# The triangular solve of an RWKV-7 time mix: summing by rows instead of updating what is left

## The chip, the cores and the metric

The kernel runs on one core of one Trainium2 chip. The core has TensorE (PE, matrix products), VectorE (DVE), ScalarE (ACT), GpSimd (POOL) and SyncE (SP, here the queue that issues the transfers). The metric is device microseconds of one execution, and the median of several runs is given.

## The reference

Two model blocks are computed one after the other for 256 tokens of width 1024, in float32: the first with attention, a gated spatial mixer and expert lookups, the second with SwiGLU layers, a parallel attention and, in its second layer, an RWKV-7 time mix. Only the last bears on the change. Its recurrence, over 16 heads of 64, is:

```
def rwkv7_step(state, inp):
    r_t, w_t, k_t, v_t, a_t, b_t = inp
    sa = jnp.einsum('bhvk,bhk->bhv', state, a_t)
    state = (state * w_t[:, :, None, :] + sa[..., None] * b_t[:, :, None, :]
             + v_t[..., None] * k_t[:, :, None, :])
    return state, jnp.einsum('bhvk,bhk->bhv', state, r_t)
```

## The kernel before, in words

The kernel does not step through 256 tokens. It cuts them into 8 chunks of 32 (`C = 32`; 4 chunks in each of two tiles of 128 tokens). Inside a chunk, what a token adds to the state depends on the earlier tokens of the chunk through a strictly triangular 32 x 32 matrix of products. For each of the 16 heads and 8 chunks, 128 systems in all, the kernel needs the inverse of identity minus that matrix. `invert` (L2237 to L2308) computes them all at once, one system on each of the 128 partitions.

The order of `invert` is written out by hand and is the same on every run. Transposes and matmuls on TensorE give the products, VectorE masks them into `sysd`. Then a block of instructions begins in which only SyncE and VectorE take part. SyncE stores `sysd` to a buffer in memory and loads it back as `sy`, now with one system a partition (L2284). VectorE meanwhile clears `XT`, writes ones on its diagonal, and clears `inv`. Then comes the solve (L2299 to L2308). `XT[p, j, t]` becomes the inverse of system p, `sy[p, i, t]` is its matrix, nonzero for i < t. The tiles are row-major with 32 float32 to a row, so neighbours in t are 4 bytes apart and neighbours in i or j 128 bytes. In the trace `sy` is called sys and `inv` is called inverseT.

Step i of the solve takes column i of `XT`, which is final by then, and adds its product with row i of `sy` to all later columns. That is one multiplication into `terms` (L2302) and one addition into `XT` (L2304). `kit.dve` makes VectorE wait for the end of an instruction before the next one starts. The last addition signals `solved`. SyncE waits for it, stores `XT` (L2286), waits for that, and loads the inverses as diagonal blocks of `inv` (four loads). All engines meet at the end of the block. Then `vector_only` clears a state (L1984), and `recur` runs twice, once for each tile of 128 tokens, with `inv` as an operand of its matmuls. `finish_mix` follows, and one more SwiGLU ends the kernel.

Of the kernel before, what the change touches and what calls it, by code (L numbers as in the profile page):

```python
# [18 lines left out]
ALU = mybir.AluOpType  # L19
ACT = mybir.ActivationFunctionType  # L20
AX = mybir.AxisListType.X

P = 128
# [30 lines left out]
C = 32  # L54
# [160 lines left out]
def transposes(kit, jobs):  # L215


    nc = kit.nc
    turned, freed = kit.count("turned"), [kit.count("turned_out_act"), kit.count("turned_out_dve")]
    b0, f0 = turned.n, [f.n for f in freed]  # L220
    with nc.Block() as block:
        @block.tensor
        def _(pe):
            for j, (ins, _) in enumerate(jobs):
                if j >= 4:
                    pe.wait_ge(freed[j % 2].sem, f0[j % 2] + (j - 4) // 2 + 1)
                n = ins[0].shape[0]
                for i, a in enumerate(ins):
                    mm = nc.tensor.transpose(kit.bank[j % 4][:, i * n:(i + 1) * n], a, kit.ident[0:n, 0:n])
                turned.up(mm)  # L230

        def source(j):
            n, t = len(jobs[j][0]), jobs[j][0][0].shape[0]
            return kit.bank[j % 4][:, 0:n * t].rearrange("p (n t) -> p n t", n=n)

        @block.scalar
        def _(act):
            for j in range(0, len(jobs), 2):
                act.wait_ge(turned.sem, b0 + j + 1)
                freed[0].up(nc.scalar.copy(jobs[j][1], source(j)))  # L240

        @block.vector
        def _(dve):
            for j in range(1, len(jobs), 2):
                dve.wait_ge(turned.sem, b0 + j + 1)
                freed[1].up(nc.vector.tensor_copy(jobs[j][1], source(j)))
# [1990 lines left out]
def invert(kit, dram, A, KK, inv):  # L2237

    nc = kit.nc
    NS = NT * RH
    grams, masked, stored, loaded, solved = (kit.count(n) for n in ("grams", "grams_masked", "systems_stored", "loaded",
                                                                    "solved"))
    g0, m0, t0, l0, v0 = grams.n, masked.n, stored.n, loaded.n, solved.n
    tri, out = (dram[n].rearrange("(u c) (j t) -> c j u t", c=CH, j=C) for n in ("systems", "inverses"))
    with kit.sb("sysd", [P, NS, C]) as sysd, kit.sb("sys", [P, C, C]) as sy, kit.sb("XT", [P, C, C]) as XT, \
            kit.sb("terms", [P, C, C]) as terms:
        with kit.sb("aT", [P, NT * KD, P]) as aT, kit.sb("bT", [P, NT * KD, P]) as bT:
            transposes(kit, [([src[:, T, (k + i) * P:(k + i + 1) * P] for i in range(4)],  # L2250
                              dst[:, T * KD + k:T * KD + k + 4, :])
                             for src, dst in ((KK, aT), (A, bT)) for T in range(NT) for k in (0, 4)])
            with nc.Block() as block:
                @block.tensor
                def _(pe):


                    for n in range(NS // 4):
                        if n >= 4:
                            pe.wait_ge(masked.sem, m0 + (n - 3) * CH)  # L2260
                        for i in range(4):
                            b, p = n % 2 * HD, n // 2 * 4 + i
                            mm = nc.tensor.matmul(kit.bank[n % 4][:, i * P:(i + 1) * P], bT[b:b + HD, p, :],
                                                  aT[b:b + HD, p, :], start=True, stop=True)
                        grams.up(mm)

                @block.vector
                def _(dve):
                    for n in range(NS // 4):
                        dve.wait_ge(grams.sem, g0 + n + 1)  # L2270
                        for c in range(CH):
                            r = slice(c * C, (c + 1) * C)
                            bank = kit.bank[n % 4][:, :].rearrange("p (u t) -> p u t", u=4)
                            u = n // 2 * 8 + n % 2
                            masked.up(nc.vector.tensor_tensor(sysd[r, u:u + 7:2, :], bank[r, :, r],
                                                              kit.lt[r, r].unsqueeze(1).to_broadcast([C, 4, C]), ALU.mult))

        with nc.Block() as block:
            @block.sync
            def _(sp):  # L2280
                for c in range(CH):
                    stored.up(sp.dma_start(tri[c], sysd[c * C:(c + 1) * C]), 16)
                sp.wait_ge(stored.sem, t0 + 16 * CH)
                kit.load(sp, sy[:], dram["systems"].rearrange("s (j t) -> s j t", j=C))  # L2284
                sp.wait_ge(solved.sem, v0 + 1)
                stored.up(sp.dma_start(dram["inverses"].rearrange("s (j t) -> s j t", j=C), XT[:]), 16)  # L2286
                sp.wait_ge(stored.sem, t0 + 16 * (CH + 1))
                for c in range(CH):
                    r = slice(c * C, (c + 1) * C)
                    kit.load(sp, inv[r, :, r], out[c])  # L2290
                sp.wait_ge(loaded.sem, l0 + 16 * (CH + 1))

            @block.vector
            def _(dve):
                kit.dve(nc.vector.memset(XT[:], 0.0))
                kit.dve(nc.vector.memset(XT[:].rearrange("p j t -> p (j t)")[:, 0::C + 1], 1.0))
                nc.vector.memset(inv[:], 0.0)
                dve.wait_ge(loaded.sem, l0 + 16)
                for i in range(C - 1):  # L2299

                    n, later = C - 1 - i, XT[:, 0:i + 1, i + 1:]
                    kit.dve(nc.vector.tensor_tensor(terms[:, 0:i + 1, 0:n], XT[:, 0:i + 1, i].unsqueeze(2).to_broadcast([P, i + 1, n]),  # L2302
                                                    sy[:, i, i + 1:].unsqueeze(1).to_broadcast([P, i + 1, n]), ALU.mult))
                    ins = nc.vector.tensor_tensor(later, later, terms[:, 0:i + 1, 0:n], ALU.add)  # L2304
                    if n > 1:
                        kit.dve(ins)
                    else:
                        solved.up(ins)  # L2308
# [326 lines left out]
```

## Time and profile before

| | |
|---|---|
| median of 3 runs | 3264.07 us (3259.56 to 3265.90) |
| the profiled execution | 3264.07 us, span 3262.2 us |
| mean granted TensorE clock | 0.895 of full speed |
| TensorE matmuls busy | 2546.1 us (78%) |
| VectorE busy | 1768.1 us (54%) |
| ScalarE busy | 1103.9 us (34%) |
| GpSimd busy | 594.6 us (18%) |

A busy share is an average over stages with different limits. What a change in one stage is worth is read from that stage: from the timeline of its stretch, and from who waits for whom there. All positions in time are microseconds from the start of the span.

### The profile page before, as it was taken

The page shows a single profiled execution, that of the slowest core. Times are in us where ns is not written, and L with a number is a line of the kernel's source. Part 1 is how long each engine was busy: PE and PEld are TensorE (multiplying, and loading weights), DVE is VectorE, ACT ScalarE, POOL GpSimd, SP SyncE. Part 2 cuts the span into 40 slices and gives each one's busy share as a digit, 9 for nine tenths or more (in the row PEclk, how much of TensorE's full clock was granted, in tenths as well). Part 3 has the DMA queues.
Part 4 walks back from the last instruction along what each step waited for, and adds up shares of the span by engine and source line. Part 5 has one row for each costly group of instructions (what it writes and reads, how often), then busy time and mean ns, then how long its engine had stood idle before and what let it go on. Part 6 is the DMA issues. An engine that isn't in the chain of part 4 may idle for free. (4 is left out here: it accounts for less than half of the span.)

```text
span 3262.2 us, 35838 instructions
## 1 busy us (share of the span) xinstructions
PE 2546.1 (78%) x13519; PEld 1769.7 (54%) x13519; DVE 1768.1 (54%) x3125; ACT 1103.9 (34%) x2207; POOL 594.6 (18%) x516
## 2 busy tenths in 40 slices
PE   6776788888874787888777988479989785285899
PEld 4554333333223333333226978359979782185798
DVE  3325866666554866666654544325544454645454
ACT  3232434444332444444334333333333241100332
POOL 0001444444420444444430000000000000000000
PEclk8877999999996999999998999669989887575899
DMA  9755999999982999999992544115535432100353
GB/s 376 272 198 213 418 421 422 421 421 419 415 342 87 419 421 421 421 421 421 421 421 101 186 168 156 42 45 181 188 140 181 160 137 80 26 1 14 114 190 116
DMA packets 134224, 817.07 MB, mean 250 GB/s; under 512 B 24863, under 2 KB 32375, under 8 KB 38348
## 3 DMA queue, kind: packets, MB, share of 16 engines
q0 software_dynamic: 73728, 536.90, 39.7%
q1 hardware_dynamic: 60364, 278.47, 23.6%
q8 instruction: 76, 1.25, 0.2%
q14 instruction: 56, 0.46, 0.0%
HBM read 813.16 MB, written 2.16 MB: 250 GB/s over the span
## 5 line engine op out<-in xcount | busy, mean ns | idle before, releaser
L1241 PE MATMUL bank<-rows,diag 128*128 128x512 f32 x2048 | 998.6, 621 | 259.6 <-ACT diag L1304 259.2
L1423 DVE CUSTOM_DVE_ANT_0 rows<-rows,h 128x1024 f32<-128x1024 f32 x512 | 623.8, 1227 | 424.1 <-DMA rows<-in_peer_rows,idx 420.3
L1241 PEld LDWEIGHTS bank<-rows,diag 128*128 128x128 f32 x2048 | 365.2, 193 | 814.3 <-ACT diag L1304 522.1
L1191 POOL DMA_INDIRECT rows<-in_peer_rows,idx x512 | 594.4, 1161 | 1113.1 <-PE bank L1241 688.6
L1627 DVE TENSOR_TENSOR low<-weight_ring,high 128x2048 fp32r<-128x2048 f32 x132 | 301.5, 2292 | 275.7 <-ACT high L1602 275.7
L1559 PE MATMUL bank<-hT_high,low 128*128 128x256 f32 x1408 | 403.4, 287 | 0.0
L1559 PE MATMUL bank<-hT_low,high 128*128 128x256 f32 x1408 | 402.8, 286 | 0.0
L1559 PE MATMUL bank<-hT_high,high 128*128 128x256 f32 x1408 | 402.7, 286 | 0.0
L1295 ACT ACTIVATE picks<-picks 128x1 f32<-128x1 f32 x512 | 103.5, 202 | 739.0 <-DVE picks L1423 733.5
L1602 ACT CAST high<-weight_ring 128x2048 fp32r<-128x2048 f32 x132 | 250.5, 1903 | 264.5 <-PE bank L1559 132.1
L1559 PEld LDWEIGHTS bank<-hT_high,low 128*128 128x128 f32 x1408 | 274.8, 195 | 7.4 <-issue 4.5
L1559 PEld LDWEIGHTS bank<-hT_low,high 128*128 128x128 f32 x1408 | 274.7, 195 | 1.4
L1559 PEld LDWEIGHTS bank<-hT_high,high 128*128 128x128 f32 x1408 | 274.5, 195 | 0.0
L1304 ACT ACTIVATE diag<-const_table,picks 128x128 f32<-128x128 f32 x512 | 205.5, 401 | 48.3 <-ACT picks L1299 1.5
L1299 ACT ACTIVATE picks<-picks 128x1 f32<-128x1 f32 x512 | 150.7, 294 | 18.5
L1217 PE MATMUL bank<-x_high,low 128*128 128x256 f32 x256 | 114.8, 449 | 29.9 <-DVE low L1334 24.5
L1574 PE MATMUL bank<-low,hidden 128*128 128x512 f32 x352 | 137.6, 391 | 0.0
L1574 PE MATMUL bank<-high,hidden_low 128*128 128x512 f32 x352 | 137.5, 391 | 0.0
L1574 PE MATMUL bank<-high,hidden 128*128 128x512 f32 x352 | 137.0, 389 | 0.0
L477 PE MATMUL bank<-low,x_high 128*128 128x256 f32 x432 | 126.3, 292 | 11.8 <-DVE low L489 11.8
L477 PE MATMUL bank<-high,x_low 128*128 128x256 f32 x432 | 124.5, 288 | 0.0
L477 PE MATMUL bank<-high,x_high 128*128 128x256 f32 x432 | 124.2, 287 | 0.0
(412 smaller groups left out, 3268.4 us busy)
## 6 DMA issues: line engine op xcount, KB each, us to landing
weight_ring<-in_ffn_w_gate SPq DMA_DIRECT2D x44, 1024.0 KB, 4.8
weight_ring<-in_ffn_w_up SPq DMA_DIRECT2D x44, 1024.0 KB, 4.8
weight_ring<-in_ffn_w_down SPq DMA_DIRECT2D x44, 1024.0 KB, 4.8
mod_ring<-in_mod_w SPq DMA_DIRECT2D x40, 1024.0 KB, 7.9
weight_ring<-in_peer_w_q SPq DMA_DIRECT2D x16, 1024.0 KB, 7.5
weight_ring<-in_attn_w_in SPq DMA_DIRECT2D x12, 1024.0 KB, 4.8
weight_ring<-in_mod_w SPq DMA_DIRECT2D x8, 1024.0 KB, 16.9
rows<-in_peer_rows,idx POOLq DMA_INDIRECT x512, 15.1
```

Of the source, the lines that this page charges most:

```text
L477: mm = nc.tensor.matmul(o, t[:, k, cols], w[:, k, :], **kw)
L1191: nc.gpsimd.indirect_dma_start(ring[:, s], None, dram["peer_rows"], bass.IndirectOffsetOnAxis(ap=idx[:, T, n:n + 1], axis=0)).then_inc(row ...
L1217: mm = nc.tensor.matmul(kit.bank[hh % 2][:, half * SEQ:(half + 1) * SEQ], w[:, k, half * P:(half + 1) * P], t[:, k, :], start=(k == 0 and ...
L1241: mm = nc.tensor.matmul(bank[:, :], diag[:, j % DIAG_SLOTS], ring[:, j % ROW_SLOTS, D + half * 512:D + (half + 1) * 512], start=(hh == 0 a ...
L1295: gelued.up(nc.scalar.activation(dot[:, T, n:n + 1], dot[:, T, n:n + 1], ACT.Gelu_apprx_tanh))
L1299: scaled.up(nc.scalar.activation(weight[:, T, n:n + 1], dot[:, T, n:n + 1], ACT.Copy, scale=gate[:, T, n:n + 1]))
L1304: weighed.up(nc.scalar.activation(diag[:, j % DIAG_SLOTS], kit.ident, ACT.Copy, scale=weight[:, T, n:n + 1]))
L1423: dotted.up(nc.vector.tensor_tensor_reduce(out=ring[:, s, 0:D], in0=ring[:, s, 0:D], in1=h[:, T], scale=1.0, scalar=0.0, op0=ALU.mult, op1 ...
L1559: mm = nc.tensor.matmul(o, w[:, k, s * P:(s + 1) * P], t[:, k, :], start=(k == 0 and n == 0), stop=(k == KD - 1 and n == 2))
L1574: mm = nc.tensor.matmul(kit.bank[4 + 2 * T + half][:, :], hidden[:, f % 2, s, T * P:(T + 1) * P], w[:, s, half * 512:(half + 1) * 512], st ...
L1602: nc.scalar.copy(hi, w).then_inc(high_made.sem, 1)
L1627: nc.vector.tensor_tensor(lo, w, hi.bitcast(F32), ALU.subtract).then_inc(split.sem, 1)
```

## The change

Step i used to update all columns behind column i. Now step t makes column t final in one go: it multiplies the finished t x t corner of `XT` with column t of `sy`, repeated down the rows, and sums the products of each row into column t of `XT`. There are still 31 multiplications, each followed by one more instruction in the same chain of waits. The second is a `tensor_reduce` along the innermost dimension in place of a `tensor_tensor`. Loads, stores, memsets and the signal `solved` are as before.

```diff
-                for i in range(C - 1):
-
-                    n, later = C - 1 - i, XT[:, 0:i + 1, i + 1:]
-                    kit.dve(nc.vector.tensor_tensor(terms[:, 0:i + 1, 0:n], XT[:, 0:i + 1, i].unsqueeze(2).to_broadcast([P, i + 1, n]),
-                                                    sy[:, i, i + 1:].unsqueeze(1).to_broadcast([P, i + 1, n]), ALU.mult))
-                    ins = nc.vector.tensor_tensor(later, later, terms[:, 0:i + 1, 0:n], ALU.add)
-                    if n > 1:
+                for t in range(1, C):
+
+                    kit.dve(nc.vector.tensor_tensor(terms[:, 0:t, 0:t], XT[:, 0:t, 0:t],
+                                                    sy[:, 0:t, t].unsqueeze(1).to_broadcast([P, t, t]), ALU.mult))
+                    ins = nc.vector.tensor_reduce(XT[:, 0:t, t], terms[:, 0:t, 0:t], AX, ALU.add)
+                    if t < C - 1:
                         kit.dve(ins)
                     else:
                         solved.up(ins)
```

The start of the solve on VectorE, before (in these rows a shape such as 128x2x30 is partitions, rows, elements of a row):

```order
L2297 MEMSET inverseT 128x4096
L2302 TENSOR_TENSOR terms<-XT,sys 128x31
L2304 TENSOR_TENSOR XT<-XT,terms 128x31
L2302 TENSOR_TENSOR terms<-XT,sys 128x2x30
L2304 TENSOR_TENSOR XT<-XT,terms 128x2x30
L2302 TENSOR_TENSOR terms<-XT,sys 128x3x29
```

And now:

```order
L2297 MEMSET inverseT 128x4096
L2301 TENSOR_TENSOR terms<-XT,sys 128x1
L2303 TENSOR_REDUCE XT<-terms 128x1
L2301 TENSOR_TENSOR terms<-XT,sys 128x2x2
L2303 TENSOR_REDUCE XT<-terms 128x2
L2301 TENSOR_TENSOR terms<-XT,sys 128x3x3
```

The blocks began wide and flat and now begin small. The shape of a reduction is that of its output; it reads as many elements as the multiplication ahead of it writes. The end of the solve, before:

```order
L2302 TENSOR_TENSOR terms<-XT,sys 128x29x3
L2304 TENSOR_TENSOR XT<-XT,terms 128x29x3
L2302 TENSOR_TENSOR terms<-XT,sys 128x30x2
L2304 TENSOR_TENSOR XT<-XT,terms 128x30x2
L2302 TENSOR_TENSOR terms<-XT,sys 128x31
L2304 TENSOR_TENSOR XT<-XT,terms 128x31
L2278 UNCONDITIONAL_BRANCH
```

And now:

```order
L2301 TENSOR_TENSOR terms<-XT,sys 128x29x29
L2303 TENSOR_REDUCE XT<-terms 128x29
L2301 TENSOR_TENSOR terms<-XT,sys 128x30x30
L2303 TENSOR_REDUCE XT<-terms 128x30
L2301 TENSOR_TENSOR terms<-XT,sys 128x31x31
L2303 TENSOR_REDUCE XT<-terms 128x31
L2278 UNCONDITIONAL_BRANCH
```

The blocks used to get narrow again and now are largest at the end. The rows around the solve, and those of all other engines, are as they were, one line of the kernel further up.

## Rows read from the trace of the kernel before

**Rows 1.** Timeline of the solve: start us, us, instruction, [idle before].
```profile
2811.30 3.47 DVE L2297 MEMSET inverseT<- 128x4096 f32 x1 [0.92 <-DVE XT L2296]
2814.10 0.34 SPq L172 DMA_DIRECT2D sys<-systems  x1
2817.31 0.19 DVE L2302 TENSOR_TENSOR terms<-XT,sys 128x31 f32<-128x31 f32 x1 [2.54 <-DMA sys<-systems]
2817.54 0.19 DVE L2304 TENSOR_TENSOR XT<-XT,terms 128x31 f32<-128x31 f32 x1
...
2840.46 0.21 DVE L2304 TENSOR_TENSOR XT<-XT,terms 128x31 f32<-128x31 f32 x1
2840.70 0.34 SPq L2286 DMA_DIRECT2D inverses<-XT  x1
2843.32 2.17 SPq L172 DMA_DIRECT2D inverseT<-inverses  x4
2849.00 0.48 DVE L1984 MEMSET states<- 128x512 f32 x1 [8.33 <-PEq L2278]
...
2849.79 0.45 PE L229 MATMUL bank<-const_table,KK 128*128 128x128 f32 x1 [44.68 <-PEq L1949]
```
**Rows 2.** The same stretch as one row of windows: length, busy by engine, clock, DMA.
```profile
2817.31:2840.67 23.36, 0.00 (x0) 0.00 (x0) 21.27 (x62) 0.00 (x0) 0.00 (x0) 0.50 0.00 0
```
**Rows 3.** Waits of SyncE and TensorE around it: us, times, longest.
```profile
SPq L2286 <- DVE XT L2304: 26.2, 1, 26.2
...
PE bank L229 <- PEq L1949: 44.7, 1, 44.7
```
**Rows 4.** Groups by shape, first step of the solve: busy us, mean ns.
```profile
L2302 DVE TENSOR_TENSOR terms<-XT,sys 128x31 f32<-128x31 f32 x1 | 0.2, 193 | 2.5 <-DMA sys<-systems 2.5
L2304 DVE TENSOR_TENSOR XT<-XT,terms 128x31 f32<-128x31 f32 x1 | 0.2, 192 | 0.0
```
**Rows 5.** Groups by shape, widest steps.
```profile
L2302 DVE TENSOR_TENSOR terms<-XT,sys 128x255 f32<-128x255 f32 x2 | 0.9, 426 | 0.1
L2302 DVE TENSOR_TENSOR terms<-XT,sys 128x256 f32<-128x256 f32 x1 | 0.4, 424 | 0.0
```
**Rows 6.** Groups by shape, reductions elsewhere in the kernel.
```profile
L1373 DVE TENSOR_REDUCE ranks<-hT 128x32 f32<-128x512 f32 x28 | 19.2, 686 | 1.0
L1373 DVE TENSOR_REDUCE ranks<-hT 128x16 f32<-128x256 f32 x8 | 3.4, 420 | 0.3
L1388 DVE TENSOR_REDUCE ranks<-picks 128x2 f32<-128x32 f32 x14 | 2.5, 181 | 0.0
L2488 DVE TENSOR_REDUCE st<-sq 128x16 f32<-128x1024 f32 x2 | 2.4, 1220 | 0.1
L1388 DVE TENSOR_REDUCE ranks<-picks 128x1 f32<-128x16 f32 x4 | 0.7, 164 | 0.0
```
**Rows 7.** Groups by shape, memsets ahead of the solve.
```profile
L2297 DVE MEMSET inverseT<- 128x4096 f32 x1 | 3.5, 3472 | 0.9 <-DVE XT L2296 0.9
L2295 DVE MEMSET XT<- 128x1024 f32 x1 | 0.9, 912 | 0.6 <-PEq L2253 0.6
L2296 DVE MEMSET XT<- 128x32 f32 x1 | 0.1, 85 | 0.1
```
**Rows 8.** Timeline of VectorE in `finish_mix`.
```profile
2996.33 1.23 DVE L2498 TENSOR_TENSOR R<-R,G 128x1024 f32<-128x1024 f32 x1
2997.59 1.22 DVE L2484 TENSOR_REDUCE st<-R 128x16 f32<-128x1024 f32 x1
2998.84 0.17 DVE L2485 TENSOR_SCALAR st<-st 128x16 f32<-128x16 f32 x1
```
**Rows 9.** Groups by shape, the last step and the addition before it.
```profile
L2304 DVE TENSOR_TENSOR XT<-XT,terms 128x60 f32<-128x60 f32 x1 | 0.2, 223 | 0.0
L2304 DVE TENSOR_TENSOR XT<-XT,terms 128x31 f32<-128x31 f32 x1 | 0.2, 212 | 0.0
L2302 DVE TENSOR_TENSOR terms<-XT,sys 128x31 f32<-128x31 f32 x1 | 0.2, 210 | 0.0
```
**Rows 10.** The addition of the second step, by shape.
```profile
L2304 DVE TENSOR_TENSOR XT<-XT,terms 128x60 f32<-128x60 f32 x1 | 0.2, 221 | 0.0
```
**Rows 11.** Windows: the two halves of the recurrence (busy PE, PEld, DVE, ACT, POOL, clock).
```profile
2849.79:2914.99 65.20, 58.71 (x769) 55.88 (x769) 27.79 (x43) 4.49 (x8) 0.00 (x0) 0.75 0.01 2
2914.99:2984.05 69.06, 62.82 (x768) 59.61 (x768) 27.88 (x43) 4.52 (x9) 0.00 (x0) 0.69 0.01 2
```
**Rows 12.** Timeline of SyncE's queue behind the solve.
```profile
2984.41 0.42 SPq L172 DMA_DIRECT2D ln<-in_rw_lnx_b  x1
3029.47 0.33 SPq L198 DMA_DIRECT2D weight_ring<-in_ffn_w_gate  x1
```

## The prediction

> **What bounds the kernel now.** I read five views in turn. First the time: the profiled execution took 3264.07 us around a span of 3262.2 us, and it is also the median of the three runs shown (3259.56 to 3265.90). So a sum made on the profile is a sum on the median. What a measurement of this kernel can tell from no change is about 0.2%, 6.5 us.
>
> Second, the timeline of the solve [rows 1]. The reader is to see a single file. VectorE is the only engine at work from 2817.31 to 2840.67 us, first mult to last add. Its first multiplication waits for the load of the systems, the last addition releases the store of the inverses, that store the four loads, those the next stage, whose first matmul starts at 2849.79. Third, the same stretch as one row [rows 2]: 23.36 us, of which VectorE is busy 21.27 in 62 instructions, with DMA share 0.00. Fourth, the waits of the store queue and of TensorE [rows 3]: SyncE waits 26.2 us for the last addition, TensorE 44.7 us at the barrier of the stage. Nothing is prefetched or multiplied beside this stretch. So a microsecond more or less on VectorE there is a microsecond of the span, whatever VectorE's 54% over the whole kernel suggests. Fifth, the durations by shape, for the prices.
>
> **The change, part by part.** Before, step i multiplies and adds a block of (i+1) x (31-i) elements per partition, for i = 0 to 30. After, step t multiplies a block of t x t and sums it by rows, for t = 1 to 31. Both have 31 multiplications and 31 second instructions in one dependent chain. Elements per pass: before, the sum of (i+1)(31-i), 5456; after, the sum of t squared, 10416. So nothing is saved in instructions, and 4960 elements are added in each of two passes.
>
> *Multiplication, fixed part and rate.* 31 elements in adjacent places take 193 ns [rows 4], 255 take 426 [rows 5]: 233/224 = 1.04 ns an element, on a fixed 161 ns. The old passes worked out by that are 2 x (31 x 0.161 + 5456 x 0.00104) = 21.33 us, against 21.27 in [rows 2], so the fit holds for every shape in between, square ones (16 x 16, 424 ns) included. The new multiplications: 31 x 0.161 + 10416 x 0.00104 = 15.82 us, if the operands' layout costs nothing.
>
> *The sum by rows.* The kernel has reductions elsewhere [rows 6]: 256 elements to 16 take 420 ns, 512 to 32 take 686, 1024 to 16 take 1220. From the first to the last that is 800/768 = 1.04 ns an element on 153 ns. Small ones lie a little under (16 to 1: 164 ns, 32 to 2: 181). Rows of 16 and of 64 have one rate, so I see no price per row. 31 x 0.153 + 10416 x 0.00104 = 15.58 us. The rows bound it on both sides to a few tenths. The sums are written down a column, every 32nd element. The nearest row for such a write is the memset of the diagonal, every 33rd element: 32 elements in 85 ns, where the memset of 1024 takes 912 and that of 4096 takes 3472, 0.83 ns an element on 59, which makes 86 for 32 [rows 7]. A strided write costs nothing there, and there is only one to t elements read.
>
> *Gaps.* Before, 23.36 - 21.27 = 2.09 us lie in the 61 gaps, 34 ns each. Elsewhere the next instruction starts some 30 ns after the end, behind a reduction as behind a multiplication [rows 8]. Again 2.1 us, within 0.3.
>
> Sum without layout: 15.82 + 15.58 - 21.27 = +10.1 us.
>
> *The column that is read.* The old multiplication reads a row of the systems, 31 neighbours. The new one reads a column of it, sy[:, 0:t, t], whose elements lie 128 bytes apart, and it is the innermost dimension. No instruction before does that at length, but the last step does it once with 31 elements. Its multiplication reads column 30 of XT and takes 210 ns, where the first step has 193 for 31 neighbours; its addition reads two columns and takes 212 for 192 [rows 4, 9]. With 30 rows of 2 there is no price: that addition takes 223 ns, against 221 with 2 rows of 30 [rows 9, 10]. I read the 17 ns as a price per element, 17/31 = 0.55 ns, about half of the normal rate again. From below: if it is a fixed start-up, 31 x 17 ns = 0.5 us in all. From above: if some of it was hidden in so short an instruction, a full second element time may be due for each, 10416 x 1.04 ns = 10.8 us. I take the nearest row, 10416 x 0.55 = 5.7 us.
> The Trainium skill has both readings. "SBUF — State Buffer", section "Door 1: The DMA port swizzle", says that two accesses to a 16-byte line are needed for full bandwidth and that each crossing to a new line costs; the trace agrees, as the 31 x 1 form pays [rows 9] and the 30 x 2 form doesn't. "VectorE: DVE Perf Modes", section "Mode 1× (REGULAR) — the baseline", says of that mode that fp32 and odd strides work and that it gives one result a cycle; by that the column is free.
>
> *The rest.* The diagonal, the memsets, the store and the four loads stay: 2840.70 to 2849.79 is only shifted. The SyncE queue holds nothing but this chain; the next weight load is issued at 3029.47 [rows 12], behind the recurrence. TensorE idles before the recurrence 16 us longer, from a granted clock already at 0.50 [rows 2], the low level of 1.2 GHz; it can't go lower there. So I price this at nothing but a shift of phase, priced below with the rivals.
>
> Forecast: 3264.07 + 10.1 + 5.7 = 3279.9 us, slower by 0.48%. The likeliest case's own range is 3276 to 3284: the two terms have some 1 us between them (20 ns instead of 17 would be 6.7 us), and the rest is the clock.
>
> **The rivals.**
>
> *A, the column is free.* The 17 ns are a start-up for strided forms, or belong to rows of one element. For it: it is one instruction of 31 elements, and the strided write is free [rows 7]. Against: the addition, with two strided reads, shows 20 ns also. The time is 3264.07 + 10.1 to 10.6, 3274.4.
>
> *B, the column costs a whole element time or more.* For it: in 31 elements some of the price can lie in the fixed 161 ns. Against: nothing was hidden in the memset, whose rate fits at 32 elements. 3264.07 + 10.1 + 10.8 = 3285 us.
>
> *C, the clock gives it back, and the kernel is faster.* The two halves of the recurrence do the same work, but took 65.20 us at a mean granted clock of 0.75 and 69.06 at 0.69 [rows 11]. So the clock's phase is worth about 4 us a half, and the change shifts that phase. To offset 15.8 us and reach -6.5, TensorE's busy time of 58.7 + 62.8 = 121.5 us would have to fall by 22.4. Taken as scaling with the clock, it is 58.7 x 0.75 + 62.8 x 0.69 = 87.4 us of full clock, so the mean clock would have to be over 87.4/99.1 = 0.88 in both halves; at 1.0 the time would be 3264.07 + 15.8 - 34 = 3246 us. Against: both halves are far under 0.88 and nothing in the change makes TensorE's work there denser. A partial case, both halves as the better one or better still, takes 4 to 8 us off, and with a free column it would end within 0.2%: about 3268.
>
> *D, the change does not do what it says*, since the stretch is hidden elsewhere: [rows 3] excludes it.
>
> **How the numbers follow.** Forecast 0.5, A 0.24, B 0.17, the partial case of C (within 0.2%) 0.07, C in full 0.02. All but C are slower by more than 0.2%: 0.91; the same 0.07; faster 0.02. Time 3280. The range takes in A with 3 us of scatter below and B: 3270 to 3287; left out are C and what lies beyond B, under 2 in 10.
>
> **What would show it.** The solve as 38 to 40 us between its first multiplication and its last sum, where there were 23.36, still 62 instructions; the store right behind. The sum over 31 x 31 elements at 1.15 us. The multiplication over 31 x 31 at 1.16 us if A holds, 1.7 if the forecast does (161 + 961 x 1.59), 2.2 with B. In the recurrence, halves of 65 to 69 us as before. I am wrong if the reductions cost per row (small t far over 0.2 us), if that stretch does not account for the difference of the spans within 5 us, or if the difference is under 6.5 us.

## The result: slower by 0.58%

The changed kernel takes 3282.35 us (median of 10 runs; 3278.45 to 3292.96 in nine of them; the tenth took 7244.23 us, for a reason that nothing here shows, and is left aside). The kernel before, run beside it, takes 3265.43 (10 runs, 3256.21 to 3274.36). The ratio is 1.0058, with a 95% interval of 1.0041 to 1.0076: 13 to 25 us slower. 3280 were forecast. The profiled execution took 3286.17 us around a span of 3284.3.

In the profile after, the solve is the same single file, only longer. The same stretch as one row of windows (length, busy PE, PEld, DVE, ACT, POOL, clock, DMA share, GB/s), to be set beside [rows 2]:

```profile
2817.65:2858.02 40.37, 0.00 (x0) 0.00 (x0) 38.26 (x62) 0.00 (x0) 0.00 (x0) 0.50 0.00 0
```

40.37 us for 23.36, so +17.0 us, with 62 instructions as before. The gaps are 40.37 - 38.26 = 2.1 us, as before. The waits that answer to [rows 3] (us, times, longest) have grown by the same amount, 17.0 and 17.5:

```profile
SPq L2286 <- DVE XT L2303: 43.2, 1, 43.2
...
PE bank L229 <- PEq L1949: 62.2, 1, 62.2
```

Its end in the timeline (start us, us, instruction, idle before) shows that what follows at once is shifted and not changed. The store follows the last sum, the loads 2.6 us later, and the first matmul comes 9.3 us behind the issue of the store, where it was 9.1 [rows 1]:

```profile
2855.03 1.79 DVE L2301 TENSOR_TENSOR terms<-XT,sys 128x961 f32<-128x961 f32 x1
2856.86 1.16 DVE L2303 TENSOR_REDUCE XT<-terms 128x31 f32<-128x961 f32 x1
2858.04 0.34 SPq L2286 DMA_DIRECT2D inverses<-XT  x1
2860.66 2.28 SPq L172 DMA_DIRECT2D inverseT<-inverses  x4
...
2867.32 0.45 PE L229 MATMUL bank<-const_table,KK 128*128 128x128 f32 x1 [62.16 <-PEq L1949]
```

The groups by line over the solve (busy us, mean ns) split the 38.26 us. Before, the two groups had 10.6 us each.

```profile
L2301 DVE TENSOR_TENSOR terms<-XT,sys 128x1 f32<-128x1 f32 (+30 forms) x31 | 22.6, 730 | 3.6 <-DMA sys<-systems 2.6
L2303 DVE TENSOR_REDUCE XT<-terms 128x1 f32<-128x1 f32 (+30 forms) x31 | 15.6, 505 | 1.1
```

The reductions are where the sum put them, at 15.6 us. The multiplications are at 22.6. The sum had 15.8 for elements in rows and 5.7 for the column. By shape:

```profile
L2301 DVE TENSOR_TENSOR terms<-XT,sys 128x961 f32<-128x961 f32 x1 | 1.8, 1789 | 0.0
L2303 DVE TENSOR_REDUCE XT<-terms 128x31 f32<-128x961 f32 x1 | 1.2, 1155 | 0.0
...
L2301 DVE TENSOR_TENSOR terms<-XT,sys 128x256 f32<-128x256 f32 x1 | 0.6, 585 | 0.0
...
L2303 DVE TENSOR_REDUCE XT<-terms 128x16 f32<-128x256 f32 x1 | 0.4, 422 | 0.0
```

A multiplication of 256 elements took 424 ns in the old 16 x 16 step [rows 5] and takes 585 now. 961 take 1789: (1789 - 161)/961 = 1.69 ns an element, where the reduction of the same block has 1.04.

The span of this execution grew by 22.1 us, not by 17.0. Of the other 5.1, 0.3 lie ahead of the solve and 4.5 between the store of the inverses and the next load on SyncE's queue, 147.82 us for 143.31. The instructions there are the same; "The clock behind the solve" below takes this up.

### The profile page after: what moved, and what is told of

Read it like the earlier page. It is cut to its first block and busy times, and to the rows that moved or that the text cites. A ratio compares the mean times of both kernels' runs of the same rounds, so it can differ in the third digit from the quotient of the medians.

```text
span 3284.3 us, 35838 instructions
## 1 busy us (share of the span) xinstructions
PE 2553.2 (78%) x13519; PEld 1775.5 (54%) x13519; DVE 1784.7 (54%) x3125; ACT 1104.5 (34%) x2207; POOL 595.5 (18%) x516
## 5 line engine op out<-in xcount | busy, mean ns | idle before, releaser
L1304 ACT ACTIVATE diag<-const_table,picks 128x128 f32<-128x128 f32 x512 | 205.5, 401 | 48.3 <-ACT picks L1299 1.5
```

Source lines behind the costliest of these rows:

```text
L1304: weighed.up(nc.scalar.activation(diag[:, j % DIAG_SLOTS], kit.ident, ACT.Copy, scale=weight[:, T, n:n + 1]))
```

## The experiments

Theory 1: the kernel is slower by what VectorE does in the solve, 10.1 us for more elements and the rest for the column, a price of about 0.65 ns for each element of an operand whose neighbours are 128 bytes apart. Rivals: the surplus belongs to the square blocks or the column write; it is a start-up for each instruction; or part of the time comes from the clock behind the solve.

In all of them the solve is read from the profile, from the first multiplication to the end of the last instruction of the solve. In the diffs, `...` stands for lines left out.

**The column taken away.** In the changed kernel the operands of the matmul that makes the systems are exchanged, and the mask is the other triangle:

```diff
-                            mm = nc.tensor.matmul(kit.bank[n % 4][:, i * P:(i + 1) * P], bT[b:b + HD, p, :],
-                                                  aT[b:b + HD, p, :], start=True, stop=True)
+                            mm = nc.tensor.matmul(kit.bank[n % 4][:, i * P:(i + 1) * P], aT[b:b + HD, p, :],
+                                                  bT[b:b + HD, p, :], start=True, stop=True)
...
-                                                              kit.lt[r, r].unsqueeze(1).to_broadcast([C, 4, C]), ALU.mult))
+                                                              kit.after[r, r].unsqueeze(1).to_broadcast([C, 4, C]), ALU.mult))
...
-                                                    sy[:, 0:t, t].unsqueeze(1).to_broadcast([P, t, t]), ALU.mult))
+                                                    sy[:, t, 0:t].unsqueeze(1).to_broadcast([P, t, t]), ALU.mult))
```

> The changed kernel, but the two operands of the matmul that makes the systems are exchanged and the mask is the opposite triangle, so that each system lies transposed in memory and the multiplication reads a row of it, sy[:, t, 0:t], 4 bytes apart. Everything else, t x t blocks and sums by rows written down a column, is as changed. Theory 1 (the column that is read costs some 0.65 ns an element, as 31 x 31 elements took 1.789 us): the multiplication over 31 x 31 falls to 1.16 us, the solve from 40.4 us to 33.5, and the time is 10 us over the kernel before. Theory 2 (the surplus over 1.04 ns an element belongs to the square blocks or to what the column write of XT leaves behind): the multiplication stays at 1.7 to 1.8 us and the solve at 40 us, 17 us over.

The solve took 33.53 us. In the window of the solve, and by shape:

```profile
2820.14:2853.67 33.53, 0.00 (x0) 0.00 (x0) 31.42 (x62) 0.00 (x0) 0.00 (x0) 0.50 0.00 0
```
```profile
L2301 DVE TENSOR_TENSOR terms<-XT,sys 128x961 f32<-128x961 f32 x1 | 1.2, 1160 | 0.0
L2303 DVE TENSOR_REDUCE XT<-terms 128x31 f32<-128x961 f32 x1 | 1.2, 1155 | 0.0
```

The multiplications fell from 22.6 to 15.8 us: the column's price is 6.8 us, 0.65 ns for each of the 10416 elements. What is left, 33.53 - 23.36 = 10.2 us, is the price of the larger blocks and of the sum in place of the addition, forecast at 10.1. The ratio to before is 1.0030 (1.0010 to 1.0051), 3 to 17 us over before, which holds 10.

**The column given to the kernel before.** The same exchange and mask in the kernel before, and a column in its multiplication:

```diff
-                                                    sy[:, i, i + 1:].unsqueeze(1).to_broadcast([P, i + 1, n]), ALU.mult))
+                                                    sy[:, i + 1:, i].unsqueeze(1).to_broadcast([P, i + 1, n]), ALU.mult))
```

> The kernel before, with the systems lying transposed (operands of the matmul exchanged, opposite mask), so that the old multiplication of step i reads a column, sy[:, i+1:, i], 128 bytes apart. Additions as before. Theory 1 (0.65 ns for each element whose operand runs down a column): 5456 x 0.65 = 3.5 us more in the solve, 26.9 for 23.4; the widest multiplication (16 x 16) takes 0.59 us for 0.42; the time is 3 to 4 us over before. Theory 2 (a start-up for each strided instruction, 17 ns): 0.5 us in all. Theory 3 (the price belongs to the square blocks of the change): nothing.

The solve took 26.90 us for 23.36, +3.5. Groups by shape at its widest steps:

```profile
L2302 DVE TENSOR_TENSOR terms<-XT,sys 128x256 f32<-128x256 f32 x1 | 0.6, 598 | 0.0
L2304 DVE TENSOR_TENSOR XT<-XT,terms 128x256 f32<-128x256 f32 x1 | 0.4, 426 | 0.0
```

The price came without the change's square blocks and without its column write, and it grew with the elements, not with the instructions (0.5 us by a start-up). The ratio to before is 1.0020 (1.0001 to 1.0038), 0 to 12 us, which holds 3.5.

**The price by itself.** 29 single instructions (the expectation says 34) behind the last addition of the kernel before, ahead of the signal. This kernel and the next were executed once each, and only durations are read from them. This is the fourth, with step 4; the other nine of the first ten differ in the slice of `fs` (`sy` as one row of elements) alone, which is `0:30*s+1:s` for a step of s:

```diff
+                kit.dve(nc.vector.tensor_tensor(ft[:, 0:248].rearrange('p (a b) -> p a b', a=8), fx[:, 0:248].rearrange('p (a b) -> p a b', a=8), fs[:, 0:121:4].unsqueeze(1).to_broadcast([P, 8, 31]), ALU.mult))
```

> The kernel before, with 34 single VectorE instructions between the last addition of the solve and the signal to the store, each waiting for the one before it; each reads sy and XT and writes the tile terms, which is not used afterwards. Ten multiplications of 8 x 31 elements (outer step 0 on the second operand, first operand and output in neighbouring places) differ only in the step of the second operand: 1, 2, 3, 4, 5, 8, 16, 31, 32 and 33 float32. Theory 1a (a price for each element that lies in another 16-byte line than the one before): step 1 0.42 us, step 2 the same, step 4 and all above 0.58, step 3 between. Theory 1b (a conflict of steps that are powers of two, or of rows of 128 bytes): 32 and perhaps 16 at 0.58, 31, 33 and 5 at 0.42. Theory 2 (a start-up for a strided form): all strided ones at 0.44. Then the column on the first operand: 0.58 by theory 1; on both: 0.58 if the two reads overlap, 0.74 if they add; on the output: 0.42, as writes looked free. 31 x 31 with step 32: 1.79 as in the changed kernel. Single columns of 4, 8, 16 elements against rows: 3, 5, 10 ns more by theory 1, 17 ns each by theory 2. tensor_copy of 8 x 31, which reads one tensor: at step 1 about 0.30 and more at step 32. The reduction over 31 x 31: 1.16 us with the sums in neighbouring places and down a column, and about 1.8 where it reads down columns.

Groups by line. L2307 to L2316 are steps 1, 2, 3, 4, 5, 8, 16, 31, 32, 33. L2318 has a column as first operand, L2319 as both, L2320 as output. L2332 and L2331 are the copy at step 32 and 1, L2335 and L2334 the sums over 31 x 31 read down columns and along rows:

```profile
L2335 DVE TENSOR_REDUCE terms<-XT 128x31 f32<-128x961 f32 x1 | 1.8, 1756 | 0.0
...
L2334 DVE TENSOR_REDUCE terms<-XT 128x31 f32<-128x961 f32 x1 | 1.2, 1155 | 0.0
...
L2311 DVE TENSOR_TENSOR terms<-XT,sys 128x248 f32<-128x248 f32 x1 | 0.6, 611 | 0.0
L2314 DVE TENSOR_TENSOR terms<-XT,sys 128x248 f32<-128x248 f32 x1 | 0.6, 607 | 0.0
L2312 DVE TENSOR_TENSOR terms<-XT,sys 128x248 f32<-128x248 f32 x1 | 0.6, 603 | 0.0
L2319 DVE TENSOR_TENSOR terms<-XT,sys 128x248 f32<-128x248 f32 x1 | 0.6, 600 | 0.0
L2316 DVE TENSOR_TENSOR terms<-XT,sys 128x248 f32<-128x248 f32 x1 | 0.6, 598 | 0.0
L2310 DVE TENSOR_TENSOR terms<-XT,sys 128x248 f32<-128x248 f32 x1 | 0.6, 595 | 0.0
L2315 DVE TENSOR_TENSOR terms<-XT,sys 128x248 f32<-128x248 f32 x1 | 0.6, 578 | 0.0
L2318 DVE TENSOR_TENSOR terms<-XT,sys 128x248 f32<-128x248 f32 x1 | 0.6, 577 | 0.0
L2313 DVE TENSOR_TENSOR terms<-XT,sys 128x248 f32<-128x248 f32 x1 | 0.6, 576 | 0.0
L2320 DVE TENSOR_TENSOR terms<-XT,sys 128x248 f32<-128x248 f32 x1 | 0.6, 574 | 0.0
L2309 DVE TENSOR_TENSOR terms<-XT,sys 128x248 f32<-128x248 f32 x1 | 0.5, 487 | 0.0
L2308 DVE TENSOR_TENSOR terms<-XT,sys 128x248 f32<-128x248 f32 x1 | 0.4, 417 | 0.0
...
L2307 DVE TENSOR_TENSOR terms<-XT,sys 128x248 f32<-128x248 f32 x1 | 0.4, 416 | 0.0
L2332 DVE COPY terms<-sys 128x248 f32<-128x248 f32 x1 | 0.4, 393 | 0.0
L2331 DVE COPY terms<-sys 128x248 f32<-128x248 f32 x1 | 0.3, 291 | 0.0
```

Steps 1 and 2 cost 416 and 417 ns, step 3 costs 487, and from step 4 (16 bytes) on it is 576 to 611, powers of two or not. So it isn't a conflict of addresses that lie 128 bytes apart. Single columns of 4, 8 and 16 elements took 5, 6 and 12 ns more than rows (166 for 161, 172 for 166, 186 for 174): it grows with the elements from the first few on. One expectation failed: the output down a column was to be free and took 574.

**Where it begins, and writes.** A second set of 16, most on 248 elements in one row of steps:

> The kernel before with 16 single instructions between the last addition and the signal to the store, all on 248 elements in one row of steps. Multiplications with the output at step 1, 2, 3, 4: if writes pay by the 16-byte line as reads do, 416, 417, 487, 575 ns; if the 574 ns of the output down a column came from the step of 128 bytes, step 4 is at 416. Second operand at step 4: 0.58 to 0.60; both inputs: 0.60; inputs and output: 0.60 if the three streams overlap, over 0.7 if reads and writes share the price. Second operand in pairs, two neighbours of every eight: if two accesses to a line make it free, 0.42; the same pairs moved by three elements, so that each pair lies across two lines: 0.58 by the line theory, 0.42 if neighbours are what counts. Memset of 248 at step 1 and step 4: 0.27 both if a memset is free of the price, as 32 elements showed, 0.43 else; 31 x 31 down columns and in rows: 0.86 both, or 1.5 for columns. tensor_copy step 1 to 1: 0.29; read at step 4: 0.39; written at step 4: 0.29 if writes are free where two elements are moved at once.

Groups by line. L2307 to L2310: output at step 1, 2, 3, 4. L2311: second operand at step 4, L2312: both inputs, L2313: all three. L2314 and L2315: pairs of neighbours that start at element 0 and at element 3 of every eight. L2316 and L2317: memset at step 1 and 4. L2318 and L2319, in the timeline further down: memset of 31 x 31 down columns and in rows. L2320 to L2322: copy with no step, read at step 4, written at step 4:

```profile
L2313 DVE TENSOR_TENSOR terms<-XT,sys 128x248 f32<-128x248 f32 x1 | 0.6, 598 | 0.0
L2311 DVE TENSOR_TENSOR terms<-XT,sys 128x248 f32<-128x248 f32 x1 | 0.6, 597 | 0.0
L2315 DVE TENSOR_TENSOR terms<-XT,sys 128x248 f32<-128x248 f32 x1 | 0.6, 597 | 0.0
L2310 DVE TENSOR_TENSOR terms<-XT,sys 128x248 f32<-128x248 f32 x1 | 0.6, 596 | 0.0
L2312 DVE TENSOR_TENSOR terms<-XT,sys 128x248 f32<-128x248 f32 x1 | 0.6, 593 | 0.0
L2309 DVE TENSOR_TENSOR terms<-XT,sys 128x248 f32<-128x248 f32 x1 | 0.5, 490 | 0.0
L2308 DVE TENSOR_TENSOR terms<-XT,sys 128x248 f32<-128x248 f32 x1 | 0.4, 418 | 0.0
L2314 DVE TENSOR_TENSOR terms<-XT,sys 128x248 f32<-128x248 f32 x1 | 0.4, 418 | 0.0
...
L2322 DVE COPY terms<-sys 128x248 f32<-128x248 f32 x1 | 0.4, 384 | 0.0
L2321 DVE COPY terms<-sys 128x248 f32<-128x248 f32 x1 | 0.4, 379 | 0.0
L2320 DVE COPY terms<-sys 128x248 f32<-128x248 f32 x1 | 0.3, 289 | 0.0
L2316 DVE MEMSET terms<- 128x248 f32 x1 | 0.3, 265 | 0.1
L2317 DVE MEMSET terms<- 128x248 f32 x1 | 0.3, 265 | 0.3 <-DVE terms L2316 0.3
```

The pairs settle what counts. The two rows differ by where the pairs lie only. At element 0 a pair shares 16 aligned bytes and costs nothing (418). At element 3 it lies across two such groups and costs as much as step 4 (597). So the price is for an element that is the only one touched in its 16 bytes before the next group is. Writes pay like reads, and a second or third strided operand adds nothing. A copy, which is faster to begin with, goes from 289 to 380 ns.

A memset seems to pay nothing, 265 ns at step 1 and 4. But the timeline shows time ahead of each one that its duration leaves out:

```profile
2839.60 0.60 DVE L2315 TENSOR_TENSOR terms<-XT,sys 128x248 f32<-128x248 f32 x1
2840.31 0.27 DVE L2316 MEMSET terms<- 128x248 f32 x1
2840.87 0.27 DVE L2317 MEMSET terms<- 128x248 f32 x1 [0.29 <-DVE terms L2316]
2842.01 0.86 DVE L2318 MEMSET terms<- 128x961 f32 x1 [0.87 <-DVE terms L2317]
2843.14 0.86 DVE L2319 MEMSET terms<- 128x961 f32 x1 [0.27 <-DVE terms L2318]
2844.03 0.29 DVE L2320 COPY terms<-sys 128x248 f32<-128x248 f32 x1
```

From the end of the instruction ahead to its own end, the memset of 248 elements took 0.38 us at step 1 and 0.56 at step 4, that of 961 took 1.73 down columns and 1.13 in rows. The surplus, 0.18 and 0.60 us, is 0.7 and 0.6 ns an element, the multiplication's price. The idle time goes with the memset behind it and not with the one ahead, since the copy starts 0.03 us behind L2319. So a memset pays too.

**Turned once.** The changed kernel with one copy ahead of the loop:

```diff
+                kit.dve(nc.vector.tensor_copy(sysd[:], sy[:].rearrange("p j t -> p t j")))
...
-                                                    sy[:, 0:t, t].unsqueeze(1).to_broadcast([P, t, t]), ALU.mult))
+                                                    sysd[:, t, 0:t].unsqueeze(1).to_broadcast([P, t, t]), ALU.mult))
```

> The changed kernel with one tensor_copy ahead of the solve that turns sy into the tile sysd, free by then, so that each column of the systems lies in a row of sysd, and the multiplications read sysd[:, t, 0:t]. The copy reads 1024 elements down columns: 248 took 393 ns, 291 with step 1, so about 0.16 + 1024 x 0.94 ns = 1.1 us; if a write in another order makes it worse, 1.8. The multiplications then fall to the row price. Theory 1 (a price for each use of a strided element, so it pays to turn once): from the issue of the load to the store 43.6 - 6.7 + 1.2 = 38.1 us. Theory 2 (price elsewhere): 44.7.

The copy took 1028 ns, the multiplications 15.8 us again, and from the issue of the load (2819.85) to the store (2857.65) it was 37.80 us for 43.59 in the changed kernel. One strided pass of 1.0 us replaced 6.8 us of strided multiplications. It is still 11.2 us over the 26.60 of the kernel before, as the blocks are as large as in the change. It was executed once, so only the stretch is read from it.

**Idle work in place of the change.** The kernel before with 18 memsets of `terms` behind the last addition:

```diff
-                    if n > 1:
-                        kit.dve(ins)
-                    else:
-                        solved.up(ins)
+                    kit.dve(ins)
+                for _ in range(18):
+                    kit.dve(nc.vector.memset(terms[:], 0.0))
+                solved.up(nc.vector.memset(kit.spare[:, 2:3], 0.0))
```

> The kernel before, with 18 memsets of the tile terms behind the last addition of the solve and ahead of the signal to the store: 18 x (0.91 + 0.04) = 17.1 us of VectorE time, none of it needed. Theory 1 (the stretch is serial and what follows is only shifted): the median is 17 us over before, as in the changed kernel. Rival C (the shift of the clock's phase gives back or adds several us in the recurrence on average): the median is off 17 by over 4 us, up or down. Rival D (part of the stretch is hidden): clearly under 17.

The pad was larger than meant, since each memset took 1.19 us from end to end, 0.28 idle and 0.91 recorded (the first too, which follows an addition): from the issue of the load to the store it was 48.26 us, 21.7 more than before. The median was 3293.76 against 3265.45, the ratio 1.0094 (1.0066 to 1.0122), 22 to 40 us. That left rival C open, so the pad was made again with multiplications along rows:

```diff
-                    if n > 1:
-                        kit.dve(ins)
-                    else:
-                        solved.up(ins)
+                    kit.dve(ins)
+                for _ in range(14):
+                    kit.dve(nc.vector.tensor_tensor(terms[:, 0:31, 0:31], XT[:, 0:31, 0:31], sy[:, 0:31, 0:31], ALU.mult))
+                solved.up(nc.vector.memset(kit.spare[:, 2:3], 0.0))
```

> The kernel before with 14 multiplications of 31 x 31 elements, all operands in rows, behind the last addition and ahead of the signal to the store: 14 x (1.160 + 0.035) = 16.7 us, and a memset of one element. In the earlier pad the memsets turned out 0.28 us apart and not 0.04, so that it was 21.7 us and its measured 28 to 31 us (interval 22 to 40) can't be held against 17. Theory 1 (what follows is only shifted): 17 us over before, the same as the changed kernel. Rival C (an idle stretch of TensorE that is longer by this much costs more in the clock afterwards, as the 28 of the pad could mean): 22 us or more.

From the issue of the load to the store it was 43.44 us, 16.8 more than before. The median was 3272.68 against 3262.85, the ratio 1.0034 (1.0013 to 1.0055): 4 to 18 us. One pad came out 9 us above its length (1.0094 is 30.7 us for 21.7), the other 6 below (11.1 for 16.8). Both lengths lie inside their intervals, but close to an end, on opposite sides: the first leaves room for 0 to 18 us above its length, the second for 13 below to 1 above. The intervals of the changed kernel (13 to 25 us for 17.0) and of the two exchanges hold their lengths as well. So a microsecond in this stretch costs about one microsecond, and no surplus or refund of the clock shows that these runs share; each alone leaves several microseconds open.

**The clock behind the solve.** The windows from the store of the inverses to the next load on SyncE's queue hold the same instructions in every kernel here. Before, changed, the second pad, and the kernel before with the column:

```profile
2840.70:2984.01 143.31, 121.53 (x1536) 115.53 (x1536) 56.15 (x87) 8.97 (x16) 0.00 (x0) 0.70 0.05 9
```
```profile
2858.04:3005.86 147.82, 125.22 (x1536) 118.95 (x1536) 56.06 (x87) 8.98 (x16) 0.00 (x0) 0.68 0.04 9
```
```profile
2860.77:2993.08 132.31, 110.09 (x1536) 104.19 (x1536) 56.05 (x87) 8.99 (x16) 0.00 (x0) 0.77 0.05 10
```
```profile
2855.16:3006.83 151.67, 129.75 (x1536) 123.53 (x1536) 56.09 (x87) 8.98 (x16) 0.00 (x0) 0.66 0.04 8
```

132.3 us at a mean clock of 0.77, 151.7 at 0.66, with VectorE's work at 56.1 in all. It does not go with how long TensorE idled: the second pad, with 43.4 us from load to store, is followed by the shortest stretch, and the first, with 48.3 us, by 140.3. So the 4.5 us that the changed kernel lost here in its profile are no more than this scatter. It is not the only part that scatters. Ahead of the load of the systems the kernels differ only in the exchanged operands and in two memsets, and the eleven profiles took 2808.6 to 2824.9 us there. Single executions of the kernel before differ by 10 us and more (3246.0 to 3277.4 in one set of 29).

**A version of the kernel before with fewer elements.** XT starts as the identity plus the systems, so that step 0 falls away and step i adds to i rows. The ones are written on the diagonal once `XT` has landed, and the products are cut to i rows too:

```diff
+                kit.load(sp, XT[:], dram["systems"].rearrange("s (j t) -> s j t", j=C))
...
-                kit.dve(nc.vector.memset(XT[:], 0.0))
...
-                for i in range(C - 1):
+                for i in range(1, C - 1):
...
-                    n, later = C - 1 - i, XT[:, 0:i + 1, i + 1:]
+                    n, later = C - 1 - i, XT[:, 0:i, i + 1:]
...
```

> The kernel before, with XT loaded with the systems themselves (a second load beside that of sy) and ones written on the diagonal once it has landed, so that step 0 falls away and step i adds to rows 0 to i-1 only: 30 multiplications and 30 additions with sum of i(31-i) = 4960 elements a pass. By the rates of the solve (161 ns an instruction, 1.04 ns an element, 34 ns a gap): 2 x (0.195 + 496 x 0.00104) = 1.4 us less, 0.12 more for the memset of the diagonal behind the load, and some tenths for the second load of 512 KB, up to 1.5 us if the two loads share the engines evenly. So the solve from the first memset to the last addition is 22.1 us for 23.4, and the stretch up to the store ends 0 to 1.3 us earlier. In the median nothing can be told from before.

The steps got shorter (10.0 + 9.9 us for 10.6 + 10.6), but the first multiplication came 5.0 us behind the issue of the load, for 3.2. From the issue to the store it was 26.98 us for 26.60: nothing gained. The ratio was 1.0014 (0.9997 to 1.0032), 1 us under before to 10 over. With a copy in place of the second load:

```diff
-                kit.load(sp, XT[:], dram["systems"].rearrange("s (j t) -> s j t", j=C))
...
+                kit.dve(nc.vector.tensor_copy(XT[:], sy[:]))
```

> As the seeded kernel, but XT is copied from sy by VectorE (1024 elements, about 0.53 ns each + 0.16 = 0.70 us) where the second load made the first multiplication start 5.0 us behind the issue of the load and not 3.2. Then ones on the diagonal, then steps 1 to 30. 1.43 us saved in the steps, 0.70 + 0.04 + 0.12 added ahead of them: from the issue of the load of the systems to the store of the inverses 26.0 us for 26.6. If the copy reads one element a cycle it is 1.2 us and the stretch is 26.5. In the median nothing can be told from before.

26.16 us for 26.60. The median is 3261.43 against 3262.85, the ratio 0.9998 (0.9986 to 1.0010). It beats the changed kernel clearly, and the kernel before by 0.4 us in its stretch, which no comparison of whole times can tell.

## Why the prediction was right, step by step

- *What bounds.* Right. The solve grew by 17.0 us, the whole by 13 to 25, and two pads of 21.7 and 16.8 us cost 22 to 40 and 4 to 18.
- *Larger blocks, +10.1 us.* Right: 10.2 with the column taken away. The rates from other lines (1.04 ns an element, 161 and 153 ns fixed) held from 1 to 961 elements. The reductions took 15.6 us for 15.58.
- *Gaps.* Right, 2.1 us.
- *The column, +5.7 us.* The mechanism was right and the size was low by a sixth: 6.8 us, 0.65 ns an element and not 0.55. The 17 ns came from a single instruction of 31 elements; the 20 ns of the addition beside it [rows 9], which the prediction put aside as 6.7 us, was the better number. The multiplication over 31 x 31 took 1.79 us for 1.7. That the choice between 0.5, 5.7 and 10.8 us came out right rested on two instructions of 31 elements; the forecast gave it one chance in two, and some of that is luck.
- *Writes down a column are free* [rows 7]. The step held for the reduction, which writes once for t elements read (1155 ns down a column, 1154 in a row), but the reading was wrong. The duration of a memset leaves out idle time that belongs to it: [rows 7] has 0.9 us ahead of the 4096 elements, and 0.92 + 3.47 us is 1.07 ns an element, not 0.85. Timed from end to end a strided memset pays, and a multiplication with a strided output takes 574 ns for 416. Had the change written its products down columns, the same reading would have missed it. The argument against rival B from the same rows falls with it.
- *Rival A, a free column.* Refuted by the two exchanges of operands. "VectorE: DVE Perf Modes" of the Trainium skill, section "Mode 1× (REGULAR) — the baseline", says that fp32 and odd strides work in that mode, at one result a cycle. The trace doesn't agree: 31 x 31 elements took 1.79 us with a step and 1.16 without. "SBUF — State Buffer" of the Trainium skill, section "Door 1: The DMA port swizzle", has 16-byte lines of which two accesses are needed for full rate. The trace agrees, with the pairs at 418 and 597 ns. The same note of the Trainium skill lets fp32 stride by four elements for free. If that takes in a step of 4, the trace doesn't agree: step 3 took 487 ns and step 4 took 595, for 416 at step 1.
- *Rival B, a full second element time.* Refuted: no strided form was slower than (611 - 161)/248 = 1.8 ns an element, and the long ones were at 1.69.
- *Rival C.* The clock's phase moves this kernel more than the prediction had from two halves of one run, 132 to 152 us for one stretch, but to both sides, and not with the length of the solve. No run shows that it made the loss or took it back.
- *The signs.* Three of the stated bounds were just overstepped. The solve took 40.37 us for 38 to 40, which is the column's 1.1 us. The first half of the recurrence took 70.9 us at a mean granted clock of 0.67 (2867.32 to 2938.24 us), for 65 to 69; the second took 67.2 at 0.73. And the solve left 5.1 us of the difference of the two spans open, where 5 was the limit. The last two are the scatter of the clock in one pair of profiles: the medians differ by 16.9 us.
- *The total.* 3280 for 3282.35 us looks closer than the sum deserves. Nine executions of the changed kernel lie from 3278 to 3293 us, and the interval for the loss is 12 us wide. The solve, 39.2 us by the sum (23.36 + 15.8) and 40.4 measured, is the real test.

## What to carry to other kernels

Count elements before instructions: summing by rows and updating the rest have the same number of instructions, but n^3/3 elements against n^3/6 a pass, and at 32 elements a side the elements of the old solve already took longer than its fixed parts (11.3 us of 21.3). Then look at the innermost step of every operand, the output too: with float32, a multiplication ran at full rate at step 1 and 2 and paid about 0.65 ns an element more from step 4 (16 bytes) on, and one copy that turns the operand, or an exchange of the operands of the matmul that makes it, takes that away. Where an operation is missing from the trace and its price is taken from another kind of instruction, time that one from end to end: the duration of a memset hid the price that the idle time ahead of it held.

## What the runs showed of the hardware that was not expected

- A strided output costs a VectorE multiplication as much as a strided input (596 and 597 ns for 416), all three strided no more than one (598).
- A pair of neighbours within 16 aligned bytes is free, the same pair across the boundary pays fully (418 against 597 ns).
- The recorded duration of a memset leaves out part of its time, which stands as idle time ahead of it and grows with it: 0.27 us for 961 elements in rows, 0.28 for 1024, 0.92 for 4096, and 0.87 for 961 down columns. Multiplications in the same chain of waits start 0.03 to 0.04 us behind the one ahead.
- The price isn't quite the same for every step: 8 x 31 elements took 611 ns at step 5 and 578 at step 32. In the solve 28 x 28 elements took 1466 ns and among the single instructions 1485. What sets these last few per cent was not tried.
